# Two edits of a one-core kernel on Trainium2: the modulation's rows are turned within its block loop, and a norm scales one tile ahead of writing

## What is computed

```python
# first model, two layers
for i in range(2):
    sh1, sc1, g1, sh2, sc2, g2 = split(silu(c) @ ada_w[i] + ada_b[i], 6)   # for c and for c_ctx; ada_w[i] is 1024 x 6144
    h = rmsnorm(x, norm1_g[i]) * (1 + sc1) + sh1
    x = x + g1 * (deltanet(h) if i == 0 else attention(h))
    h = rmsnorm(x, norm2_g[i]) * (1 + sc2) + sh2
    x = x + g2 * peer(h)          # gathers rows of a table of 16384 experts
x = rmsnorm(x, final_g)
# second model, two layers: x += mixer(norm(x)); x += conv_ffn(norm(x)); x += sigmoid(norm(x) @ Wg) * (p @ Wp)
```

## Time and profile before

| what | value |
|---|---|
| median of three runs | 4498.67 us (4496.3 to 4502.88) |
| the profiled execution | 4497.38 us; its span 4495.6 us |
| mean granted TensorE clock | 0.925 of full speed |
| PE busy | 3690.5 us (82% of the span) |
| DVE busy | 2567.7 us (57%) |
| POOL busy | 1257.5 us (28%) |
| ACT busy | 968.4 us (22%) |
| DMA | 1043.49 MB, mean 232 GB/s |
| chain that ended last, by engine | PE 50%, DMA 26%, DVE 13%, ACT 4%, issue 4%, POOL 3% |

### The profile page before, as it was taken

How to read it: one execution, slowest core, us unless ns; L and a number is a source line. 1 busy time by engine, 2 the same in 40 slices (tenths; PEclk the granted TensorE clock), 3 DMA queues, 4 the chain that set the end, 5 groups by cost and what they waited for, 6 DMA issues and landing times.

```text
span 4495.6 us, 59218 instructions
## 1 busy us (share of the span) xinstructions
PE 3690.5 (82%) x22791; PEld 1999.6 (44%) x22791; DVE 2567.7 (57%) x5869; ACT 968.4 (22%) x2601; POOL 1257.5 (28%) x1271
## 2 busy tenths in 40 slices
PE   6798889888979987777777778887777889865998
PEld 2446754577444442222222235443222468432683
DVE  1245643565366677776777645667775339357341
ACT  0133311333032222222222213222222120010100
POOL 1004410233023444444444400344443000036000
PEclk6698899998999999999999989999999889976999
DMA  9410012100279999999999942999999324320443
GB/s 371 145 56 13 3 48 66 48 4 3 74 287 403 414 417 420 417 415 408 413 412 408 420 146 91 401 417 419 414 415 390 106 79 140 117 70 10 134 150 122
DMA packets 269478, 1043.49 MB, mean 232 GB/s; under 512 B 19394, under 2 KB 103596, under 8 KB 170896
## 3 DMA queue, kind: packets, MB, share of 16 engines
q0 software_dynamic: 114736, 815.52, 44.6%
q1 hardware_dynamic: 154464, 224.18, 14.8%
HBM read 1038.55 MB, written 1.08 MB: 231 GB/s over the span
## 4 chain that ended last, share of the span: by engine, by line
PE 50%; DMA 26%; DVE 13%; ACT 4%; issue 4%; POOL 3%; another core or an unknown queue 0%; DVEq 0%; POOLq 0%; ACTq 0%; SPq 0%
DMA arena<-in_peer_uv,arena 24%; PE psum L261 13%; PE psum L1726 11%; PE psum L299 4%; PE psum L723 4%; PE psum L1684 3%; PE psum L762 2%; DVE arena L1861 2%; PE psum L212 2%; DMA arena<-in_ada_w 2%; PE psum L1155 1%; POOL arena L2911 1%; POOL arena L1819 1%; PE psum L1064 1%; PE psum L1075 1%
## 5 line engine op out<-in xcount | busy, mean ns | idle before, releaser
L1726 PE MATMUL psum<-arena 128*128 128x512 f32 x3072 | 1451.9, 617 | 400.4 <-ACT arena L1761 394.7
L1861 DVE SCALAR_TENSOR_TENSOR arena<-arena 128x1024 bf16<-128x1024 f32 x768 | 941.1, 1225 | 522.8 <-DMA arena<-in_peer_uv,arena 490.6
L1819 POOL DMA_INDIRECT arena<-in_peer_uv,arena x768 | 865.9, 1127 | 1174.0 <-PE psum L1726 1025.5
L1726 PEld LDWEIGHTS psum<-arena 128*128 128x128 f32 x3072 | 569.8, 194 | 1231.8 <-ACT arena L1761 642.7
L261 PE MATMUL psum<-ring,arena 128*128 128x512 f32 (+2 forms) x1408 | 595.4, 586 | 24.9 <-DVE arena L2740 9.2
L261 PEld LDWEIGHTS psum<-ring,arena 128*128 128x128 f32 x1408 | 270.3, 200 | 344.4 <-issue 317.8
L1754 ACT ACTIVATE arena<-arena 128x2 f32<-128x2 f32 x384 | 78.2, 204 | 1247.1 <-DVE arena L1861 1247.1
L299 PE MATMUL psum<-arena,ring 128*128 128x256 f32 x1408 | 314.2, 385 | 9.1 <-DVE arena L2735 7.7
L1761 ACT ACTIVATE arena<-consts,arena 128x128 f32<-128x128 f32 x768 | 268.4, 394 | 223.9 <-DVE arena L1873 219.5
L299 PEld LDWEIGHTS psum<-arena,ring 128*128 128x128 f32 x1408 | 270.0, 193 | 51.2 <-issue 8.0
L212 PE MATMUL psum<-consts,arena 128*128 128x128 f32 (+3 forms) x705 | 118.4, 315 | 139.0 <-DVE arena L362 76.2
(11 more groups left out here) (400 smaller groups left out, 4020.2 us busy)
## 6 DMA issues: line engine op xcount, KB each, us to landing
arena<-in_ada_w SPq DMA_DIRECT2D x48, 1024.0 KB, 14.4
ring<-in_ffn_w_up SPq DMA_DIRECT2D x44, 1024.0 KB
ring<-in_dn_w_in SPq DMA_DIRECT2D x24, 1024.0 KB
ring<-in_peer_w_query SPq DMA_DIRECT2D x22, 1024.0 KB
ring<-in_ffn_w_down SPq DMA_DIRECT2D x20, 1024.0 KB
arena<-in_peer_uv,arena POOLq DMA_INDIRECT x768, 12.9
ring<-in_ev_w_in SPq DMA_DIRECT2D x10, 1024.0 KB
ring<-in_dn_w_out SPq DMA_DIRECT2D x8, 1024.0 KB
```

Of the source, the lines that this page charges most:

```text
L1726: m = e.matmul(k.banks[4 + t % 2 * 2 + nh], self.diag[g % self.ND], self.vsl[g % self.NS][:, nh * 512:(nh + 1) * 512], start=u % 8 == 0 an ...
L1819: e.indirect_dma_start(self.uv[g % self.NS], None, self.table(), bass.IndirectOffsetOnAxis(ap=self.eid[u % 6][:, s:s + 1], axis=0)).then_i ...
L1861: e.scalar_tensor_tensor(self.junk[g % 2], self.us[g % self.NS], 1.0, self.h[:, u // 8, :], MUL, MUL, accum_out=self.a[u % 2][:, s:s + 1]) ...
```

## The change

In `Modulation`: a layer's weight blocks take turns in three banks instead of four, and the fourth holds the turned columns. `pe_block(n)` turns, after block n's own matmuls, the four pieces of block n-1 if that block has columns to turn (`kinds`; blocks 4, 5, 10 and 11 hold gates only), and in block 1 it first waits for the bias and transposes it. DVE makes the columns after its copy of block 10. What is left for the finish is the four gate matmuls and one add on all 128 partitions, for which POOL clears the bias tiles `gb` at the head of Ada, ahead of its bias loads. Ada has no `stores` any more: in their place POOL waits for layer 0's gate stores at the head of DeltaNet, and DVE for both layers' at job 14 of its first half. In `Norm`: DVE scales tile n+1 ahead of writing tile n, for every n; it waits then for the transposes of tile n-1.

```diff
@@ Norm.dve
-        for n, t in enumerate(self.tiles):
-            if n >= 2:
-                e.wait_ge(*st.P.at(("nt", n - 2, 1)))
-            if n == 0:
-                e.wait_ge(*V.now())
-            e.tensor_scalar(self.xn[n % 2], st.k.X[:, t, :], self.var[:, n:n + 1], None, MUL).then_inc(*V.up(("n_x", n)))
+        e.wait_ge(*V.now())
+        self.dve_scale(e, 0)
+        for n in range(len(self.tiles)):
+            if n + 1 < len(self.tiles):
+                if n:
+                    e.wait_ge(*st.P.at(("nt", n - 1, 1)))
+                self.dve_scale(e, n + 1)
             e.wait_ge(*st.P.at(("nt", n, 1)))
@@ Modulation
     def bank(self, n):
-        return self.banks[n % len(self.banks)]
+        return self.banks[n % 3]
+
+    def kinds(self, n):
+        if n in (4, 5, 10, 11):
+            return []
+        kind = n // 2 if n < 4 else n // 2 - 1
+        return [(kind * 8 + n % 2 * 4 + c, n * 512 + c * 128) for c in range(4)]
@@ pe_block, behind the block's matmuls
+        if n == 1:
+            e.wait_ge(*self.lb.at("b"))
+            self.st.turn(e, self.banks[3][:, 64:112], self.bias[0:48, :])
+        if n and self.kinds(n - 1):
+            e.wait_ge(*self.st.V.at(("row", l, n - 1)))
+            for q, o in self.kinds(n - 1):
+                m = e.matmul(self.banks[3][:, 2 * q:2 * q + 2], self.rows[:, o:o + 128], self.sel[:, 0:2], start=True, stop=True)
+            m.then_inc(*P.up(("turned", l)))
@@ dve_block
+        if n == 10:
+            self.dve_cols(e)
@@ pe_finish
-        e.wait_ge(*self.lb.at("b"))
         e.wait_ge(*V.at(("row", l, 11)))
-        self.st.turn(e, b[:, 64:112], self.bias[0:48, :])
-        for kind, o in enumerate((0, 1024, 3072, 4096)):
-            for c in range(8):
-                q = (kind * 8 + c) * 2
-                m = e.matmul(b[:, q:q + 2], self.rows[:, o + c * 128:o + (c + 1) * 128], self.sel[:, 0:2], start=True, stop=True)
-        m.then_inc(*P.up(("turned", l)))
-        e.wait_ge(*V.at(("cols", l)))
@@ dve_finish
-        e.wait_ge(*P.at(("gates", l)))
-        for j, w, h, o in self.gate_rows():
-            s = slice(32 * j, 32 * j + 2)
-            e.tensor_tensor(self.gr[s, :], b[s, :], self.gb[s, :], ADD).then_inc(*V.up(("gates", l)))
+        e.wait_ge(*self.st.P.at(("gates", l)))
+        e.wait_ge(*self.lb.at("b"))
+        e.tensor_tensor(self.gr, self.banks[0], self.gb, ADD).then_inc(*V.up(("gates", l)))
@@ Ada
-        self.stores = list(k.gates)
@@ Ada.pool
+        for mod in self.mods:
+            e.memset(mod.gb, 0.0).then_inc(*self.G.up())
+        e.wait_ge(*self.G.now())
@@ DeltaNet.pool, ahead of its first load
+        e.wait_ge(*k.gates[0].at("all"))
@@ DeltaNet.dve, job 14
+            if half == 0:
+                e.wait_ge(*self.k.gates[0].at("all"))
+                e.wait_ge(*self.k.gates[1].at("all"))
```

More of the change, by code:

```diff
@@ L371, in dve, with dve_scale @@
                 m.then_inc(*V.up(("nT", n)))
+    def dve_scale(self, e, n):
+        st = self.st
+        e.tensor_scalar(self.xn[n % 2], st.k.X[:, self.tiles[n], :], self.var[:, n:n + 1], None, MUL).then_inc(*st.V.up(("n_x", n)))
     def pe(self, e):
@@ L500, in pe_block @@
         k, P, l = self.st.k, self.st.P, self.l
-        if n >= len(self.banks):
-            e.wait_ge(*self.st.V.at(("row", l, n - len(self.banks))))
+        if n >= 3:
+            e.wait_ge(*self.st.V.at(("row", l, n - 3)))
         for k0 in (0, 4):
@@ L530, in pe_finish, with dve_cols @@
         m.then_inc(*P.up(("gates", l)))
-    def dve_finish(self, e):
+    def dve_cols(self, e):
         k, P, V, l = self.st.k, self.st.P, self.st.V, self.l
-        m, b = k.mod[:, l], self.banks[0]
+        m, b = k.mod[:, l], self.banks[3]
         e.wait_ge(*P.at(("turned", l)))
@@ L545, in dve_finish @@
                 e.scalar_tensor_tensor(m[:, kind, :, v], m[:, kind, :, v], 1.0, k.vec(name, l), ADD, MUL).then_inc(*V.up())
-        e.wait_ge(*P.at(("gates", l)))
-        for j, w, h, o in self.gate_rows():
-            s = slice(32 * j, 32 * j + 2)
-            e.tensor_tensor(self.gr[s, :], b[s, :], self.gb[s, :], ADD).then_inc(*V.up(("gates", l)))
+    def dve_finish(self, e):
+        V, l = self.st.V, self.l
+        e.wait_ge(*self.st.P.at(("gates", l)))
+        e.wait_ge(*self.lb.at("b"))
+        e.tensor_tensor(self.gr, self.banks[0], self.gb, ADD).then_inc(*V.up(("gates", l)))
     def pool_store(self, e):
```

## The result

The changed kernel takes 4438.48 us (median of four runs, 4430.15 to 4439.44) against 4500.77 of before in the same set: a ratio of 0.9864, 95% interval 0.9851 to 0.9878, about 61 us less. I had forecast 47.6 us less and 4443 to 4457. The profiled execution took 4438.26 us.

What follows compares the result with a forecast made beforehand. DMA was taken to bound the modulation's loads and PE what follows; 22.7 us from the modulation, 12.2 from four-tile norms and 12.7 from two-tile norms made 47.6 us less: 4451.0 us, range 4443 to 4457.

Steps and rivals of the forecast that it cites:

- The first layer's finish: Modulation, layer 0: turning moves into the blocks, so the loads' stall goes; 2.55 us gained.
- the turning in the loop: Modulation's blocks: turning adds 1.73 us, making 5.15 us a block against a load period of 5.43; cost 0.
- the bias wait: Block 1 of layer 0: PE waits some 1.2 us for the last bias load, covered by the loads' lead; cost 0.
- The bound on the turning: Modulation's blocks with columns: at 5.61 us against 5.43, four in a row fall 0.7 us behind; bound 2 us.
- the rival that rested on it: Modulation: turning makes PE the bound, behind at the last block and giving back 2 to 4 us; 4454 us, 9%.
- The second layer's finish: Modulation's end: 14.67 us of turning and columns, 2.15 of adds, 3.36 of store wait go; DeltaNet begins at 147.24.
- The norm with four tiles: DeltaNet and Attention: last tile starts 6.1 us after the first instead of 12.25; 6.1 us each, 12.2 together.
- The norm with two tiles: EvenMixer, Ffns, Ples, S5: PE's idle time ahead of the second tile goes; 12.7 us in all.
- I forecast the same for transposes: Norms: a TensorE kept busy by transposes stays at 1.2 GHz, as it did with narrow matmuls; no clock gain counted.
- the clock rises sooner: Norms and matmuls behind: busier PE raises the clock, 6.8 us off the gates' projection, some 9 in all; 4442, 8%.
- Scaling beside POOL: DeltaNet's norm: scaling collides with POOL's work, 1.03 us for each of three scalings on the path; 4454 us, 5%.

Runs made afterwards that it cites:

- the doubled turning: The changed kernel with each block's four turning matmuls done twice, same result; a single execution took 4436.73 us.
- the filling of transposes: The kernel before, its norm order kept, with eight transposes (results overwritten) in PE's wait for the next tile; 4477.61 us, ratio 0.9958.
- the filling of narrow matmuls: The kernel before, its norm order kept, with four two-column matmuls in PE's wait for the next tile; 4492.29 us, ratio 0.9984.
- the norm alone: The kernel before with only the norm's new loop; 4461.35 us, ratio 0.9925.
- the modulation alone: The changed kernel with the norm's loop of before, leaving only the modulation's edit; 4469.11 us, ratio 0.9945.
- unwarmed: Without the one to three 512-column matmuls added at the changed kernel's norm heads except Ple's; with them 4427.0 and 4433.1 us, with four in Ffn and S5 4426.82.

## Why the prediction was wrong, point by point

- **The first layer's finish, the turning in the loop, the bias wait.** Right: the last load is used at 141.70 (forecast 141.6), so the 2.55 us of stall are gone; 386 GB/s in the window where it was 293; the cost of the turning 0. The wait on the bias was 0.71 us and covered. The bound on the turning (5.61 us against 5.43) was too careful, and the rival that rested on it fell; the doubled turning shows that there was a margin and that it ends before 2 x.
- **The second layer's finish.** Right: every term is in its place within 0.1 us. That the sum is right to 0.02 us (147.22 against 147.24) is luck, since other executions differ by up to 1.4 us.
- **The norm with four tiles.** Order right (6.0 us to the last tile, forecast 6.1). Undersized by 1 us each, 7.05 and 7.1, since the last transposes ran at 2.4 GHz (1.1 us instead of 1.97).
- **The norm with two tiles.** 12.7 forecast, 14.4 measured; S5 and Ffn 1 gave 2.3 instead of 1.85, EvenMixer and Ffn 0 0.3 more, Ple what was forecast. In EvenMixer and Ffn 0 this isn't the clock: the sixteen transposes ran at 1.2 GHz, and in one row they take 3.65 us where two rows of eight took 1.94 + 1.97 = 3.91; this 0.6 us of the excess is an overlap that my sum left out. In S5 and Ffn 1 they took 3.45 and 3.44 us, the last of them at 2.4 GHz.
- **What failed is one step:** "I forecast the same for transposes", that is, that the transposes of the norm, now close together, would leave the clock at 1.2 GHz as the narrow matmuls of the earlier trace rows did. The changed norms show the rise in their middle, and the filling of transposes raised the clock with the old order, while the filling of narrow matmuls did not. From it follow the terms that I had at zero: Attention's whole stage from norm to Peer gave 158.6 - 149.6 = 9.0 us for a forecast of 6.1 (148.9 to 149.8 in four other executions of its code, 151.2 with the norm alone), and the six stages from EvenMixer to the end 994.9 - 973.6 = 21.3 us for a forecast of 12.7 (972.5 to 975.6 in five other executions with the new norm; 994.1 and 995.5 with the narrow filling and with the modulation alone). That is 2.9 + 8.6 = 11.5 us. It is as much as the whole excess because the other stages cancel: DeltaNet's and Peer's gave 4 us more than forecast, within their scatter, and from the second Peer to EvenMixer it took 4 us longer, in this profile alone (721.6 us, against 715 to 717.5 in the twelve others). The filling run has the mechanism in these same stages, but only 3.6 + 3.5 = 7.1 us of it; whether the rest needs the new order is open.
- **The rival "the clock rises sooner"** was the right one. I gave it 8% and 4442, and cut the range at 4443; the measured 4438.48 lies below even its price. The price was wrong in its parts: the gates' projection, from which I took 6.8 us, fell back to 1.2 GHz within 1.5 us of its start and gained 1 us; the short stages, which I put at "a few", gained most. The Trainium skill (TensorE: Matmul & The Clock Gate, Part 4) says that transpose mode doesn't engage the full clock; here the transposes of the long norms were granted it (1.09 us for eight at a granted clock of 1.00, against 1.97 at 0.50), so the measurement decides against it. Part 1 of the same page of the Trainium skill says that sustained activity releases the lower clock. The filling run agrees; the gates' projection doesn't, which was busy 13.63 of 13.70 us at 0.50.
- **Scaling beside POOL.** The rival was wrong on the path and right beside it. DeltaNet's first scaling took 0.83 us against 0.75 while POOL was issuing a load, 0.08 us on the path; in EvenMixer the second took 1.52 us beside POOL's issues, under the cover of the first tile's transposes.
- **What the 7.7 us of "rest" are.** Of them 8.55 lie in EvenMixer, the Ffns and Ples. The other executions bear out their sum together with the norms (the 21.3 above) but not each part. EvenMixer's repeats in the main (150.9 to 153.3 with the new norm, 153.1 to 154.9 without it), and so do Ple 0's and Ffn 1's. Ffn 0's 1.25 doesn't: its rest is 259.1 to 259.3 us in the other executions of the changed kernel, against 259.3 before. Ple 1's 1.7 is the profile of before, since three other executions with the old order have 1.7 us less there; and -1.8 in S5 is so too, since its 208.1 us stand against 209 to 211 in the unwarmed others. DeltaNet's 3.1 are within the scatter of the stages with Peer. Attention's -2.2 are 1.9 gained ahead of Peer and 4.1 lost behind it, the latter in this profile alone. That this scatter comes from when the granted clock rises and falls is argued from the table above, not shown: no run sets it.

## What to carry to other kernels

Price a change in PE's idle time twice: once for the time itself, and once for the clock of what stands behind it; ask which instructions fill the stretch, and look for rows where such instructions ran. Here 64-column matmuls ran at a granted clock of 0.50 for 13.7 us, and it was wrong to let them speak for transposes, during which it rose to 1.00. Moving small products into a DMA-bound loop was free here, at an estimated 5.15 us of work in a block against a load period of 5.43, and one execution with the work doubled told how near the edge is. When a single set shows a gain of 0.2% or so, put both kernels into one set before believing it.

## What the runs showed of the hardware

In Attention's norm a TensorE that was busy 12.33 of 15.7 us with transposes and two-column matmuls stayed at 1.2 GHz, while one busy 9.50 of 13.9 us with transposes alone rose to 2.4 GHz within the norm. The same program differs by 12 us in the length of one stage of some 1070 us, with the half-rate time in it between 172 and 195 us, so that a gain or loss of a few us at a stage's head can't be told from that scatter in a few runs.
